# A 31-tap causal convolution moved wholly to TensorE, as products with block-diagonal tap matrices over 4 token phases

## The reference, cut to what is computed

```
mod = silu(c) @ mod_w[l] + mod_b[l]                      # six vectors of 1024 for each layer
h = rms_norm(x, norm_g[0, 0]) * (1.0 + sc_m) + sh_m

def conformer_conv(h, w1, b1, dw, dwb, ln_g, ln_b, w2, b2):
    u = h @ w1 + b1                                      # 1024 -> 2048
    a, gt = jnp.split(u, 2, axis=-1)
    u = a * jax.nn.sigmoid(gt)
    u = causal_dwconv(u, dw, dwb)                        # y[t] = sum_j dw[j] u[t-30+j] + dwb, each channel alone
    u = jax.nn.silu(layer_norm(u, ln_g, ln_b))           # over the 1024 channels of a token
    return u @ w2 + b2
```

## Time and profile before

| | us |
|---|---|
| median of 3 runs | 2181.92 |
| lowest and highest | 2179.69, 2186.03 |
| profiled execution | 2182.34 |
| its span | 2180.5 |
| TensorE busy, share of the span | 2080.8, 95% |
| VectorE busy | 1343.5, 62% |
| ScalarE busy | 869.6, 40% |
| GpSimd busy | 156.4, 7% |
| share of TensorE in the chain that ended last | 82% |

### The profile page before, as it was taken

One profiled execution on the slowest core, in us unless ns is written; L12 is line 12 of the kernel. 1 busy time (PEld: TensorE's weight loads), 2 busy tenths in 40 slices (PEclk: granted clock), 3 DMA queues, 4 the chain that ended last, 5 costly groups with the idle time before them and its releaser, 6 DMA issues.

```text
span 2180.5 us, 26178 instructions
## 1 busy us (share of the span) xinstructions
PE 2080.8 (95%) x10575; PEld 1660.1 (76%) x10575; DVE 1343.5 (62%) x2282; ACT 869.6 (40%) x1454; POOL 156.4 (7%) x105
## 2 busy tenths in 40 slices
PE   5999999999999999899999999999888999999998
PEld 4755868888887886676888887788666788888886
DVE  7698468856844556647775566547876565624532
ACT  3455534423433245534442343333266533422421
POOL 0464100000010000020000000000000000000000
PEclk9999999999999999999999999999999999999999
DMA  8343225665531220012233323222213122333331
GB/s 300 128 149 111 72 72 187 201 202 184 179 101 59 70 86 30 30 58 64 97 100 115 101 92 102 73 84 81 63 44 114 52 83 91 97 97 96 97 97 68
DMA packets 67112, 225.01 MB, mean 103 GB/s; under 512 B 7216, under 2 KB 8112, under 8 KB 66992
## 3 DMA queue, kind: packets, MB, share of 16 engines
q1 hardware_dynamic: 64112, 218.11, 31.0%
q10 hardware_dynamic: 2880, 5.24, 0.7%
HBM read 215.98 MB, written 7.34 MB: 102 GB/s over the span
## 4 chain that ended last, share of the span: by engine, by line
PE 82%; DVE 10%; ACT 4%; issue 3%; DMA 0%; POOL 0%; SPq 0%; DVEq 0%; POOLq 0%; ACTq 0%
PE bank L288 23%; PE bank L290 22%; PE bank L289 22%; PE bank L293 14%; DVE wlo L328 1%; ACT whi L315 1%; DVE sc L2083 1%; PE bank L815 1%; DVE steps L2081 1%; ACT pr L788 1%; DVE pr L780 0%; DVE tmp L544 0%; DVE Hl L549 0%; ACT sc L788 0%; POOL small L524 0%
## 5 line engine op out<-in xcount | busy, mean ns | idle before, releaser
L288 PE MATMUL bank<-Hh,whi 128*128 128x512 f32 x1632 | 655.7, 402 | 25.2 <-DVE wlo L328 9.9
L290 PE MATMUL bank<-Hh,wlo 128*128 128x512 f32 x1632 | 641.5, 393 | 0.0
L289 PE MATMUL bank<-Hl,whi 128*128 128x512 f32 x1632 | 640.7, 393 | 0.0
L328 DVE TENSOR_TENSOR wlo<-stg,whi 128x1024 fp32r<-128x1024 f32 (+1 forms) x299 | 358.8, 1205 | 419.3 <-ACT whi L315 418.7
L315 ACT ACTIVATE whi<-stg 128x1024 fp32r<-128x1024 f32 (+1 forms) x309 | 312.9, 1025 | 416.9 <-PE bank L290 408.9
L288 PEld LDWEIGHTS bank<-Hh,whi 128*128 128x128 f32 x1632 | 310.0, 190 | 95.9 <-DVE wlo L328 11.5
L290 PEld LDWEIGHTS bank<-Hh,wlo 128*128 128x128 f32 x1632 | 309.1, 189 | 65.9
L289 PEld LDWEIGHTS bank<-Hl,whi 128*128 128x128 f32 x1632 | 310.1, 190 | 62.1 <-issue 1.5
L288 PE MATMUL bank<-HIDh,whi 128*128 128x512 f32 x352 | 141.6, 402 | 0.0
L289 PE MATMUL bank<-HIDl,whi 128*128 128x512 f32 x352 | 138.0, 392 | 0.0
L290 PE MATMUL bank<-HIDh,wlo 128*128 128x512 f32 x352 | 138.0, 392 | 0.0
(11 more groups left out here) (294 smaller groups left out, 2765.3 us busy)
## 6 DMA issues: line engine op xcount, KB each, us to landing
raw<-in_mod_w SPq DMA_DIRECT2D x96, 512.0 KB, 4.2
stg<-in_ffn_in SPq DMA_DIRECT2D x88, 512.0 KB, 3.8
stg<-in_ff SPq DMA_DIRECT2D x64, 512.0 KB, 3.5
stg<-in_ffn_out SPq DMA_DIRECT2D x40, 512.0 KB, 3.6
stg<-in_cm_w SPq DMA_DIRECT2D x24, 512.0 KB, 3.6
stg<-in_gates SPq DMA_DIRECT2D x16, 512.0 KB, 3.5
stg<-in_z_ch SPq DMA_DIRECT2D x12, 512.0 KB, 3.5
bias_kept<-out_b ACTq DMA_DIRECT2D x20, 256.0 KB, 2.1
```

The lines of the kernel that those rows point to most:

```text
L288: pe.e.matmul(out_, l[0], r[0], start=start, stop=False, skip_group_check=True)
L289: pe.e.matmul(out_, l[0], r[1], start=False, stop=False, skip_group_check=True)
L290: return pe.e.matmul(out_, l[1], r[0], start=False, stop=stop, skip_group_check=True)
L328: hand.e.tensor_tensor(wlo[j % NW][:, 0:n * c], stg[j % NSTG][:, 0:n * c], whi[j % NW][:, 0:n * c].bitcast(F32), ALU.subtract).then_inc(*m ...
```

## The change

All eight tiles are convolved on TensorE. The tokens of a tile are put in four phases (token 4j + f is column j of phase f), and the 128 channels are taken as 32 channels x 4 phases on the partitions: for a group g of 32 channels, partition (f, c) holds phase f of channel 4c + g. An output phase is then a sum over 9 shifts of a product with a 128 x 128 matrix that has nonzero numbers only where input and output channel agree. VectorE makes the nine matrices of a tile's group as one instruction of 128 x 1152 (`tap_blocks`, a row of taps times a 0/1 pattern, both operands broadcast), in four buffers `TB`; block n is 4 x tile + group, and it waits for TensorE's use of block n - 4. In this document a "phase" of the convolution on TensorE is the work on one block: 9 products of 128 columns. `conv_dve`, the diagonal matrices and the five tiles' tap steps on VectorE go.

The rows of taps are laid out once: GpSimd copies 31 sets of 8 columns, SP stores them to DRAM and loads them back shifted. `U` is stored in phase order; SP stores each tile to DRAM and loads it back as `XP` (`u_out`, `u_in`). ScalarE copies the finished sum to `CP` and stores it from its own queue (`conv_act`), SP loads it back to `C` (`c_in`). The mean now uses two tiles. Tokens stay in phase order until the evacuation of the last product of the block, which reads them back in order. ScalarE gates tiles 0 to 3 ahead of its split of block 9, and takes the modulation steps in groups of three behind tiles 0 to 3 and of four ahead of tiles 4 to 6.

```diff
-CONV_PE = (3, 5, 7)
-LAST = (6, 7)
+PHASES = 4
+GROUP = P // PHASES
+SHIFTS = (CONV - 1 + PHASES - 1) // PHASES + 1
+ROW = PHASES * SHIFTS + PHASES
+MEAN_OF = 2
...
+            U, C = sb("U", [P, DT, S], F32, ph), sb("C", [P, DT, S], F32, ph)
+            XP = [sb(f"XP{i}", [P, PHASES, SHIFTS - 1 + P], F32, ph) for i in range(4)]
+            CP = [sb(f"CP{i}", [P, S], F32, ph) for i in range(2)]
+            TB = [sb(f"TB{i}", [P, SHIFTS * P], F32, ph) for i in range(4)]
+            NT = PHASES * SHIFTS
+            rows = TB[3][:, 0:DT * ROW].rearrange("p (t l) -> p t l", l=ROW)
+            conv_w = sb("conv_w", [P, PHASES, DT * ROW], F32, ph)
+            same = sb("same", [P, GROUP], F32, ph)
...
+                sp.wait_ge(*pool_done["rows"])
+                sp.e.dma_start(w_kept.rearrange("p (t l) -> p t l", l=ROW), rows[:, :, :]).then_inc(s_rows, 16)
...
+                for f in range(PHASES):
+                    a = PHASES - 1 - f
+                    sp.e.dma_start(conv_w[GROUP * f:GROUP * (f + 1), :, 0:DT * ROW - PHASES],
+                                   w_kept[:, a:a + DT * ROW - PHASES].rearrange("(c g) l -> c g l", g=PHASES)).then_inc(s_taps, 16)
...
+                for t in range(4):
+                    u_out(t)
+                    if t:
+                        u_in(t - 1)
+                u_in(3)
...
+                for t in range(4):
+                    c_in(t)
+                    if t < 2:
+                        u_in(t + 4)
+                    aside([mods] * 3)
                 beside_gemm(sp, "cm_w1", 0, DT, 2)
+                for t in (6, 7):
+                    u_out(t)
+                for t in (6, 7):
+                    u_in(t)
+                for t in range(4, DT):
+                    if t < 7:
+                        aside([mods] * 4)
+                    c_in(t)
...
+            def u_out(t):
+                sp.wait_ge(*dve_done["u", t])
+                sp.e.dma_start(u_kept[t].rearrange("f p j -> p f j"), by_phase(U[:, t, :])).then_inc(s_u[t], 16)
+
+            def u_in(t):
+                sp.wait_ge(s_u[t], 16)
+                sp.wait_ge(*pool_done["pad"])
+                if t >= 4:
+                    sp.wait_ge(*core_done["conv", 4 * (t - 4) + 3])
+                sp.e.dma_start(XP[t % 4][:, :, SHIFTS - 1:], u_kept[t].rearrange("f (c g) j -> (f c) g j", g=PHASES)).then_inc(
+                    s_u[t], 16)
+
+            def c_in(t):
+                sp.wait_ge(s_cv[t], 16)
+                sp.e.dma_start(by_phase(C[:, t, :]), c_kept[t].rearrange("f p j -> p f j")).then_inc(s_cv[t], 16)
...
+                pool.e.memset(rows[:, :, :], 0.0).then_inc(*pool_done.up())
+                pool.wait_ge(*pool_done.now)
+                pool.wait_ge(s_vec, 16)
+                for lag in range(CONV):
+                    pool.e.tensor_copy(rows[:, :, PHASES - 1 + lag], vcol("cm_dw", 8 * (CONV - 1 - lag), DT)).then_inc(
+                        *pool_done.up(*(["rows"] if lag == CONV - 1 else [])))
+                for x in XP:
+                    tok = pool.e.memset(x[:, :, 0:SHIFTS - 1], 0.0).then_inc(*pool_done.up(*(["pad"] if x is XP[-1] else [])))
...
+                for j in LO_BY_POOL[:7]:
                     split_lo(j)
-                for l, ch, k in products[:10]:
+                for l, ch, k in products[:12]:
                     mod_product(l, ch, k)
-                for j in LO_BY_POOL[6:]:
+                gather("ln", 1)
+                gather("ln", 2)
+                for j in LO_BY_POOL[7:]:
                     split_lo(j)
-                for l, ch, k in products[10:]:
-                    mod_product(l, ch, k)
-                gather_six("ln")
+                for n in range(3):
+                    for l, ch, k in products[12 + 4 * n:16 + 4 * n]:
+                        mod_product(l, ch, k)
+                    gather("ln", 3 + n)
...
             def conv_pe(t, then={}):
                 b = acc_bank(("conv", t), [(act_done, ("conv", t))])
-                pe.wait_ge(*dve_done["u", t])
-                pe.wait_ge(*pool_done["pad"])
-                for k in range(CONV):
-                    pe.wait_ge(*act_done["tap", t, k])
-                    mm(b[:, :], dtap[k % 4][:, :], U[:, t, k:k + S], k == 0, k == CONV - 1).then_inc(*core_done.up(("tap", t, k)))
-                    if k in then:
-                        then[k]()
+                pe.wait_ge(s_u[t], 32)
+                for g in range(PHASES):
+                    n = PHASES * t + g
+                    pe.wait_ge(*dve_done["taps", n])
+                    for d in range(SHIFTS):
+                        tok = mm(b[:, g * P:(g + 1) * P], TB[n % 4][:, d * P:(d + 1) * P],
+                                 XP[t % 4][:, g, SHIFTS - 1 - d:SHIFTS - 1 - d + P], d == 0, d == SHIFTS - 1)
+                    tok.then_inc(*core_done.up(("conv", n)))
+                    if g in then:
+                        then[g]()
...
+                second_half(2)
+                for t in range(3):
+                    conv_pe(t)
+                mean()
+                conv_pe(3, {0: lambda: spread("mean", [(dve_done, ("less", DT - 1))], SPREAD, var4, dve_done["var", "mean"])})
+                second_half(3)
+                conv_pe(4)
+                less_sums(2)
+                conv_pe(5)
+                less_sums(3)
+                conv_pe(6)
+                less_sums(4)
+                conv_pe(7, {1: lambda: less_sums(5)})
+                tile_sums(part, pool_done["gathered", "ln", 5], False, False)
+                for t in (6, 7):
+                    less_sums(t)
+                    token_sums(sq[t % 4], act_done["sq", "ln", t], 0, False, t == 7, "sum" if t == 7 else "part", "ln", t)
...
+            def tap_blocks(t):
+                dve.wait_ge(s_taps, 16 * PHASES)
+                dve.wait_ge(*dve_done["same"])
+                for g in range(PHASES):
+                    n = PHASES * t + g
+                    if n >= 4:
+                        dve.wait_ge(*core_done["conv", n - 4])
+                    dve.e.tensor_tensor(TB[n % 4][:, :].rearrange("p (x c) -> p x c", c=GROUP),
+                                        conv_w[:, g, ROW * t:ROW * t + NT].unsqueeze(2).to_broadcast([P, NT, GROUP]),
+                                        same[:, :].unsqueeze(1).to_broadcast([P, NT, GROUP]), ALU.mult).then_inc(*dve_done.up(("taps", n)))
...
+                dve.e.scalar_tensor_tensor(by_phase(U[:, t, :]), phases(bank(a)[:, :]), vcol("cm_b1", t), phases(tmp[t % 4][:, :]),
+                                           ALU.add, ALU.mult).then_inc(*dve_done.up(("u", t)))
...
+                same_channel()
+                tap_blocks(0)
                 for t in range(4):
                     make_u(t)
                 for j in range(2, 4):
                     beside_gemm(dve, "cm_w1", 0, DT, 2)
-                for t, then in ((0, (4, 5)), (1, ()), (2, (6, 7)), (4, ())):
-                    all_of(conv_dve(t))
-                    for u in then:
-                        make_u(u)
-                last = conv_dve(LAST[0])
-                next(last)
-                begin_norm("mean", len(early) * P, 0.0)
-                next(last)
+                make_u(4)
+                make_u(5)
+                for t in range(1, 4):
+                    tap_blocks(t)
+                begin_norm("mean", MEAN_OF * P, 0.0)
+                tap_blocks(4)
                 dve.wait_ge(*norm_done["spread", "mean"])
-                for t in early:
-                    dve.wait_ge(*conv_ready(t))
+                for t in range(4):
                     less(t)
-                all_of(last)
-                for t in LAST:
-                    dve.wait_ge(*conv_ready(t))
+                make_u(6)
+                make_u(7)
+                tap_blocks(5)
+                tap_blocks(6)
+                less(4)
+                tap_blocks(7)
+                for t in range(5, DT):
...
+                dve.wait_ge(*conv_ready(t))
+                dve.e.scalar_tensor_tensor(C[:, t, :], C[:, t, :], vcol("cm_dwb", t), banks[SPREAD][:, :], ALU.add, ALU.subtract).then_inc(
+                    *dve_done.up(("less", t)))
...
             def conv_act(t):
-                taps(t, range(4, CONV))
-                act.wait_ge(*core_done["tap", t, CONV - 1])
-                act.e.activation(C[:, t, :], bank(("conv", t))[:, :], ACT.Identity, bias=vcol("cm_dwb", t)).then_inc(
-                    *act_done.up(("conv", t)))
+                act.wait_ge(*core_done["conv", PHASES * t + PHASES - 1])
+                if t >= 2:
+                    act.wait_ge(s_cv[t - 2], 16)
+                act.e.activation(CP[t % 2][:, :], bank(("conv", t))[:, :], ACT.Copy).then_inc(*act_done.up(("conv", t)))
+                act.wait_ge(*act_done["conv", t])
+                act.e.dma_start(c_kept[t].rearrange("f (c g) j -> (f c) (g j)", g=PHASES), CP[t % 2][:, :]).then_inc(s_cv[t], 16)
...
+                for i in (2, 4, 4, 6):
```

(50 more changed lines are left out.)

111 lines of the change are left out of this document (38 added, 73 removed).

## The result

The changed kernel takes 2195.84 us (median of 6 runs, 2189.79 to 2196.9) against 2182.18 before (6 runs, 2177.11 to 2186.03): ratio 1.0065, 95% interval 1.0052 to 1.0079, slower by 14 us. The forecast was 2189, range 2172 to 2203. The profiled execution is the quickest of the six, 2189.79 with a span of 2187.9; the time in it is compared with the 2182.3 of before.

A forecast was written before the change was run, and what follows sets the result against it. TensorE and VectorE, both nearly full, were taken to bound the convolution stage; with VectorE-GpSimd turns it ends at 226 against 220.7, 5.3 us later, plus 1.6 for the clock: 6.9 slower, 2189 us, range 2172 to 2203.

The forecast's parts named there:

- (1) The gates: ScalarE's gates ahead of the weight split: the 2.7 us TensorE gap near 76 goes, first weight half ends at 97.6, 4.2 gained.
- (2): TensorE's convolution: 576 instructions at 0.111 us, a phase 2.0 us, a tile 8.0, all 64 us against 80 before.
- (3): VectorE swaps 150 tap steps for 32 tap blocks, each 1.35 us alone and 1.27 in a row, 41 us in all.
- (4) The turns: GpSimd's modulation products and VectorE's two-SBUF-input tap blocks alternate: 3.53 us a turn against the 2.0 TensorE needs per phase.
- (5) The sum: Convolution stage added up under turns: second weight half at 148.9, last product 214.4, end 226 against 220.7; 6.9 us slower with clock.
- Centring 0.7 and two sums of 0.9 give 226: Last step of the stage's sum: from tile 7 back at 223.6, VectorE's centring and TensorE's closing sums end at 226.
- the clock 1.6 us at one start: Allowance added for TensorE starting once on the lower clock, since it now has pauses: 1.6 us, making 5.3 into 6.9.
- the copies of tiles 6 and 7 stand behind the last product: ScalarE's queue at the stage's end: these copies follow GpSimd's last product at 214.4 and are done at 218.4.
- (6) A hop: A conv tile's trip to DRAM and back, otherwise costed at nothing, exposed once at the end: 2.6 to 4.5 us.
- (7) The start: GpSimd's 31 small copies ahead of the first power: 6 us in all, taken as 0 delay; about 2 by the port lock.
- Rival A: Turns don't bind and TensorE leads the convolution stage: 22 us gained, 2160.5, if a turn costs under 2.0 us; chance 0.12.
- rival C: Much slower: start copies at 1 us give 2208, or TensorE at half clock through the convolution gives 2224; chance 0.12.

The follow-up runs named there:

- experiment 1: Changed kernel with the 0/1 pattern copied once into PSUM, so tap blocks of tiles 1 to 7 have one SBUF input: 2165.39 us, ratio 0.9926.
- experiments 1 to 5: Changed kernel with pattern in PSUM 0.9926, no GpSimd products 0.9912, paired tap blocks 1.0021, halved products 1.0037; kernel before with VectorE's running sum in SBUF 1.0301.
- experiment 8: Changed kernel plus unused TensorE products, 22 ahead of the closing sums and 18 in the wait within tile 7: 2194.02 us, ratio 1.0056.
- experiment 10: The changed kernel run again, unedited: 2194.97 us, ratio 1.0066 to the kernel before.
- Experiment 11: Changed kernel with two tap blocks per VectorE instruction, plus ScalarE's copies of conv tiles 4 to 7 ahead of its row sums: 2176.33 us, ratio 0.9981.
- experiment 12: Changed kernel with the pattern in PSUM, and tile 7's store to DRAM and load back left out: 2166.06 us, ratio 0.9934.

## Why the prediction was right, and where its terms were off

**(1) The gates** come true: no gap near 76, the convolution starts at 98.05 for 97.6. **(2)** A phase takes 2.0 us at full clock (216 instructions in 24.28 in experiment 1). **(3)** A block alone is 1.36 for 1.35.

**(4) The turns** are the cause. Forecast 3.53 a turn, measured 3.41 to 3.43; experiments 1 to 5 show it from both sides and in both kernels. The Trainium skill (SBUF — State Buffer, section SBUF: two separate sides) calls the port pair an exclusive lock, and each of these runs agrees.

**(5) The sum.** The second weight half starts at 149.6 for 148.9, the last product ends at 214.26 for 214.4, and tile 7 is ready for centring at 224.16 for 223.6. The step that failed is the last one, "Centring 0.7 and two sums of 0.9 give 226". From the centring of tile 6 at 223.40 to the end of the sums it took 7.8 us, to 231.22. Two things were missing. The row sums of tiles 6 and 7 both stand there, four groups and not two, as in the kernel before (from 216.99 to 220.7). And TensorE, idle before, ran them at the granted clock of 0.50, 1.75 us a group, where experiment 8 has 0.9. I had given the clock 1.6 us at one start. With 231.2 in place of 226 and without the 1.6 the sum is 2182.3 + 10.5 = 2192.8. The first profiled execution was 2189.8 all the same, since its later stages were 3.1 us quicker; that it met my 2189 is in this part luck. The run of experiment 10, without that, has 2182.3 + 11.7 = 2194.0 for its 2194.25. The medians are 13.7 and 15.2 us above those of the kernel before on their chips, where the two traces have a stage that is 10.5 and 11.7 us longer; the other 3 to 4 us neither trace shows.

The forecast's step within (5), that the copies of tiles 6 and 7 stand behind the last product, holds for tile 6 (215.34, right behind it). Tile 7's waited 1.28 us longer for TensorE, whose tile 7 had run in part at the lower clock (0.70 on the mean from 212.1 to 218.3) after the 4.57 us pause that ended at 210.45. I had looked for TensorE to wait in tile 7 for blocks; it waited there for tile 5's centring, and for blocks in tile 6 (up to 1.15 us each). Experiment 11 shows that the order of copies and row sums costs 8.6 us where blocks come quicker.

**(6) A hop** from the end of tile 7's copy to its centring is 224.16 - 218.84 = 5.3 us, I had 5.2 with the issues. Tile 6's is 223.40 - 215.92 = 7.5: its store took 4.4 us where I had 2.6. This I did not see, and it is why tile 6 comes back together with tile 7 and its two groups of sums are still to be done. Not seen by me either: VectorE's U in phase order costs 1.13 us where it took 0.76; I find no wait that it lengthens, since its own wait for the gates is far longer.

**(7) The start** is 0.18 us later. GpSimd's copies there (one line of the changed kernel: ns min/median/max, and when they start), and the power behind them:

```profile
L1063 POOL COPY TB<-columns x31: 192/197/1252, 5.5 to 12.7; 128x8 f32<-128x8 f32 x31
```

```profile
18.14 1.92 POOL L533 TENSOR_TENSOR small<-small 128x4 f32<-128x4 f32 x1 [5.05 <-DVE small L513]
```

The median of 0.197 is the 0.2 that I took, but the longest has 1252 ns. Two windows tell when (the fifth busy time is GpSimd's):

```profile
5.40:7.00 1.60, 0.00 (x0) 0.00 (x0) 0.00 (x0) 0.00 (x0) 1.54 (x13) 1.00 1.04 384
7.00:8.20 1.20, 0.00 (x0) 0.00 (x0) 1.16 (x2) 0.00 (x0) 1.20 (x3) 1.00 0.97 382
```

Thirteen copies fit in 1.6 us with VectorE idle, three in the 1.2 us of its first reduction over two SBUF tiles: a copy takes turns as well. So the same rule of the Trainium skill (SBUF — State Buffer, section SBUF: two separate sides) holds for a copy, which no row of before could show; the 2 us that I worked out by it did not come, because the copies began at 5.5 and were done by 12.9, 5 us ahead of the power.

**Rival A** fell by its condition, a turn below 2.0 us. Experiment 1 makes that condition true and gives 2165.4 where A had 2160.5: its closing sums end at 205.5, not 199, with tile 6 late and the lower clock again. Of **rival C** the half clock came in part: 3.4 us in the closing sums alone.

## What to carry to other kernels

Before a VectorE operation is put on a path, count its SBUF inputs and look at what GpSimd does at that time. With two SBUF inputs each of VectorE's instructions waited here for a whole one of GpSimd's: put one operand in PSUM (30 us here for one small copy), and if that can't be, make VectorE's instructions long and GpSimd's short (11 and 7 us here). Where a result goes through a queue that also serves a slow engine, put the copy that others wait for first, and price short one-column products at the clock that TensorE has after its pause.

## What was not expected of the hardware

VectorE's U reads its two inputs, one in PSUM and one in SBUF, in steps of four elements and writes in a row: 1.13 us for 512 columns, where all in order take 0.76. Which of the two reads costs it was not tried. A multiplication of 1152 with one operand broadcast from PSUM takes 1.35, the same as from SBUF. The same 256 KB store to DRAM takes 2.0 to 2.5 us or 4.1 to 4.5 within one kernel, and up to 7.9 in experiment 12.
